# Block 0 of a hybrid decoder layer: the place of the first exponents on ScalarE and of the first own pairs on TensorE

## The reference

```python
q = (xb @ w_query).reshape(L, PEER_HEADS, 2, PEER_QUERY_DIM // 2)
s = jnp.einsum('lhpd,hpkd->lhpk', q, sub_keys)
vals, idx = lax.top_k(s, K)                       # 16 best of 128, per head and side
cand = (vals[..., 0, :, None] + vals[..., 1, None, :]).reshape(L, PEER_HEADS, K * K)
best, pos = lax.top_k(cand, K)
expert = jnp.take_along_axis(cidx, pos, axis=-1)  # 8 heads x 16 = 128 experts per token
gate = jax.nn.softmax(best, axis=-1)
h = jax.nn.gelu(jnp.einsum('ld,lhkd->lhk', xb, expert_u[expert]), approximate=False)
return jnp.einsum('lhk,lhkd->ld', (h * gate), expert_v[expert])
```

## Time and profile before

| | |
|---|---|
| median of 3 runs | 3099.26 us (3098.27 to 3103.0) |
| the profiled execution | 3094.55 us |
| its span | 3092.7 us |
| mean granted TensorE clock | 0.871 |
| TensorE busy | 2367.8 us (77%) |
| VectorE busy | 2240.8 us (72%) |
| ScalarE busy | 1122.2 us (36%) |
| GpSimd busy | 1195.3 us (39%) |
| moved by DMA | 1235.90 MB, mean 400 GB/s |

### The profile page before, as it was taken

The page is one execution under the profiler, slowest core; times in us unless marked ns, Lnnn a source line. Parts: engine busy times, 40 slices in busy tenths (PEclk is TensorE's granted clock), DMA queues, the critical chain, the costliest instruction groups (busy, mean ns, idle before and its releaser), DMA issues.

```text
span 3092.7 us, 37897 instructions
## 1 busy us (share of the span) xinstructions
PE 2367.8 (77%) x11834; PEld 1335.1 (43%) x11834; DVE 2240.8 (72%) x5649; ACT 1122.2 (36%) x3540; POOL 1195.3 (39%) x1028
## 2 busy tenths in 40 slices
PE   8987878868798677877878778876878767785655
PEld 7773435534366343543446443542435424251111
DVE  5577656986679766797668966699656976678745
ACT  4224533254323633235322353224523353323222
POOL 0024452344423444234532344334543344434442
PEclk9999889889889898998989898998988879787777
DMA  8289999999999999999999999999999999999998
GB/s 350 75 339 418 421 420 409 398 414 420 420 415 413 410 420 420 402 404 418 421 419 403 414 420 421 413 394 413 418 420 406 418 413 420 420 372 421 412 421 338
DMA packets 189144, 1235.90 MB, mean 400 GB/s; under 512 B 21768, under 2 KB 21896, under 8 KB 54800
## 3 DMA queue, kind: packets, MB, share of 16 engines
q0 software_dynamic: 147456, 1073.81, 84.1%
q1 hardware_dynamic: 39312, 154.58, 12.7%
q10 hardware_dynamic: 2176, 5.10, 0.4%
HBM read 1229.21 MB, written 4.19 MB: 399 GB/s over the span
## 4 chain that ended last, share of the span: by engine, by line
DVE 29%; PE 29%; DMA 27%; ACT 7%; issue 6%; POOL 3%; DVEq 0%; SPq 0%; POOLq 0%; ACTq 0%
DMA ring<-in_uv,expert_used 26%; PE expert_sum L1048 13%; DVE ring L1920 13%; PE bank L627 7%; POOL ring L553 3%; PE bank L634 2%; ACT diag L1392 2%; PE bank L616 2%; DVE conv L1554 1%; DVE arena L1534 1%; DMA chunk<-in_weights 1%; ACT arena L1183 1%; DVE arena L1853 1%; DVE arena L1856 1%; PE bank L765 1%
## 5 line engine op out<-in xcount | busy, mean ns | idle before, releaser
L553 POOL DMA_INDIRECT ring<-in_uv,expert_used x1024 | 1195.1, 1167 | 1866.8 <-PE expert_sum L1048 1421.3
L1048 PE MATMUL expert_sum<-ring,diag 128*64 128x512 f32 x4096 | 1195.0, 713 | 632.4 <-ACT diag L1392 631.0
L1920 DVE CUSTOM_DVE_ANT_0 ring<-ring,x_pair 128x1024 f32<-128x1024 f32 x1024 | 1227.6, 1222 | 487.7 <-DMA ring<-in_uv,expert_used 482.6
L1048 PEld LDWEIGHTS expert_sum<-ring,diag 128*64 128x64 f32 x4096 | 312.5, 155 | 1258.3 <-issue 1243.9
L1385 ACT ACTIVATE h_raw<-h_raw 128x2 f32<-128x2 f32 x512 | 104.2, 204 | 1452.2 <-DVE h_raw L1920 1451.6
L1392 ACT ACTIVATE diag<-const,h_raw 128x64 f32<-128x64 f32 x1024 | 292.7, 333 | 8.1 <-PE expert_sum L1048 8.1
L1388 ACT ACTIVATE h_raw<-h_raw,gate_used 128x1 f32<-128x1 f32 x1024 | 245.6, 286 | 16.7
L627 PEld LDWEIGHTS bank<-oT,chunk 128*128 128x128 f32 x1344 | 152.7, 192 | 22.7 <-issue 22.7
L627 PE MATMUL bank<-oT,chunk 128*128 128x128 f32 x1344 | 158.6, 277 | 0.0
L1534 DVE MAX8 arena<-arena 128x8 f32<-128x128 f32 (+1 forms) x384 | 104.2, 325 | 25.9 <-ACT arena L1331 19.8
L616 PE MATMUL bank<-chunk,oT 128*128 128x256 f32 x464 | 110.7, 389 | 0.0
(11 more groups left out here) (289 smaller groups left out, 2655.9 us busy)
## 6 DMA issues: line engine op xcount, KB each, us to landing
chunk<-in_weights SPq DMA_DIRECT2D x228, 512.0 KB, 8.6
ring<-in_weights SPq DMA_DIRECT2D x17, 1024.0 KB, 23.4
ring<-in_uv,expert_used POOLq DMA_INDIRECT x1024, 15.3
chunk<-in_weights SPq DMA_DIRECT2D x4, 1024.0 KB, 20.0
x<-in_x SPq DMA_DIRECT2D x8, 512.0 KB, 13.9
o_cat<-in_xT SPq DMA_DIRECT2D x7, 512.0 KB, 14.5
out<-oT ACTq DMA_DIRECT2D x7, 512.0 KB, 9.0
xT_even<-in_xT SPq DMA_DIRECT2D x4, 512.0 KB, 10.8
```

Source lines behind the costliest of these rows:

```text
L553: pool.indirect_dma_start(out=place(n, j), out_offset=None, in_=io["uv"], in_offset=bass.IndirectOffsetOnAxis(ap=expert_used[:, j:j + 1], ...
L1048: mm = pe.matmul(expert_sum[i][c * SPAN:(c + 1) * SPAN, :], diag[:, (j % DIAGS) * SPAN:(j % DIAGS + 1) * SPAN], place(n, j)[:, D + i * 512 ...
L1920: dve.tensor_tensor_reduce(u, u, x_pair[:, (j % 2) * D:(j % 2 + 1) * D], 1.0, 0.0, ALU.mult, ALU.add, h_raw[:, j:j + 1]).then_inc(dotted.s ...
```

## The change

Two edits, both for block 0 only. On ScalarE the exponents of the first 32 slots move from behind the fifth piece's key-score copy to ahead of the fourth's. On TensorE the own pairs of block 0 are taken at the same mark as on the other engines (b in place of b - 1), with 14 pairs as the most, so that the number of pairs added at the end of block 0 stays 14, as `after_own` (L1070) says for the later blocks.

```diff
@@ TensorE @@
             taken = [0]
-            mix(0, Marks(own=lambda a, b: experts(0, b - 1)), lambda n: None, early=True)
-            after_own = taken[0]
+            after_own = sum(OWN.values()) - 1
+            mix(0, Marks(own=lambda a, b: experts(0, min(b, after_own))), lambda n: None, early=True)
@@ ScalarE @@
                 mark("more0")
                 queries_out(later + 1)
                 mark("sel0")
+                if n == 0:
+                    exponents(1, slice(0, PART))
                 key_scores_out(later + 1)
                 mark("rest0")
                 if n:
...
                 queries_out(later + 2)
                 mark("pick0")
                 key_scores_out(later + 2)
-                if n == 0:
-                    exponents(1, slice(0, PART))
                 mark("top1")
```

## The result

The changed kernel takes 3108.55 us (median of 16 runs, 3100.26 to 3113.05) against 3099.59 us for the kernel before in the same runs (16 runs, 3092.76 to 3107.16). The ratio is 1.0023, 95% interval 1.0014 to 1.0033: 7.1 us slower (4.3 to 10.2). The forecast was 2 us slower: the direction held, the size did not. The result is 5.1 us above the forecast. Counted from no change it is 0.23%, just over the bound of 0.2%, and so in the part "slower", which had a chance of 0.16. 3099.26 x 1.0023 = 3106.4 us lies in the stated range of 3092 to 3108; the median itself, 3108.55, is half a microsecond above it.

The account below looks back on a forecast made before the run. DMA, full from the fifth slice on, was taken as the bound; a 7.9 us head start is given back in smaller gaps, leaving DMA 1 to 3 us behind, taken as +2: 3099.26 + 2 = 3101 us, range 3092 to 3108.

Parts of the forecast that it names:

- the six waits: Block 0's input pass: TensorE stands still for ScalarE's diagonals at six marks, 3.1 or 1.8 us each, 13.4 us together.
- pair 0 at 168.3: Start of block 0's input pass: TensorE can start own pair 0 at 168.3 us, 7.3 us earlier than before.
- the full clock behind its wait: TensorE's own pair 0 in block 0 runs at 2.4 GHz after standing still, 1.94 us in place of 3.68.
- What bounds the kernel: Whole kernel: DMA is full from the fifth slice on; its 9.8 us of idle time near the change is the most winnable.
- rival (b): First front of block 1: the pass's delay is not hidden and costs the whole 8.1 us, so 3107; chance 0.09.
- The prediction's sign of being wrong: DMA's share in the trace after: staying 1.0 from 172 to 270 us, or under 1.0 between 275 and 300.
- Part 1: ScalarE, block 0: earlier exponents cost nothing and end VectorE's 10.37 us wait; the last key-score copy and Gelu load come late next.
- Part 2: TensorE, block 0's input pass: pairs taken at VectorE's mark, 5.3 us ahead, then 13.4 of stalls; pair 13 ends at 276.6, not 268.5.
- rival (c): Block 0's input pass: the six stalls make TensorE's clock fall to 1.2 GHz, 10 us more on the pass, 3109; chance 0.06.
- What DMA makes of it: Gathers in block 0's input pass: DMA idles 14.0 us against 11.0, no gap until 186.1 after the first gathers; taken as +2.
- (a): Gathers in block 0's input pass: the gaps do not arise, the head start stays, 8 us kept gives 3091; chance 0.10.
- (d): Block 0: the TensorE edit does nothing by itself; the exponents alone bring at most 7 us, 3092; chance 0.07.

Follow-up runs that it names:

- the last version: The changed kernel with ScalarE making block 0's pairs ahead of its copies and TensorE taking none at mark top1: 3086.56 against 3101.52 us for the kernel before, ratio 0.9944.
- the second trace: The changed kernel, unedited, traced once more as a single execution: span 3098.7 us, DMA idle 15.5 us over 170 to 290 us.

## Why the prediction came out as it did

The direction came out for the reason given, the six waits. The size did not, and three steps failed, all in the reckoning of the start: pair 0 at 168.3, the full clock behind its wait, and no DMA idle time ahead of its places. All three made the changed kernel look faster than it is.

**What bounds the kernel**: right. The span of the profiled executions follows DMA's idle time one for one (the table). So block 1's later start cost nothing beyond it, and rival (b), a price for the delay of the pass as such, fell: the run with the TensorE edit alone delays the pass most (pair 13 ends at 293.4) and still lies on the same line. The prediction's sign of being wrong, a share under 1.0 between 275 and 300, did not come: the changed kernel has 1.00, 1.00, 0.99, 1.01 and 1.02 in the five windows of 5 us. What was too low is the bound on what can be won, 9.8 us: the last version won 17.4 (13.6 to 21.1). The bound was read from one execution of the kernel before, which lay 4.7 us below its median and had less idle time than the second one.

**Part 1**: right in kind. The exponents follow the fourth query copy without a wait of ScalarE; VectorE's idle time there fell from 10.37 to 1.81 us rather than to nothing, since that copy itself came at 157.04 and not 154.28, behind the gaps. What is late next was ScalarE's last key-score copy and the Gelu load, as forecast. The table load at 169.98 took 1.28 us and was followed by the first activation at 171.28. The Trainium skill ("ScalarE: Activation LUTs", What ACT_TABLE_LOAD costs) adds a drain of about 1.38 us to the load at every switch of tables; it does not show here either.

**Part 2**: the six waits were right in place and size (13.6 against 13.4 us). The step that failed is the start: "Pair 0 can start at 168.3" and "I take the full clock". Pair 0 started at 172.61, 4.3 us later, and took 3.68 us, at the half clock; pair 5 fell to the half clock too (3.62 us). So pair 13 ended at 278.10 + 5.37 = 283.5 and not at 276.6: 4.3 us for the start, 1.7 for pair 0's clock, 1.7 for pair 5's and some 0.4 for the step behind pair 0 and the six waits make 8.1, of which about 1 came back in shorter waits for weights (2.1 us against 3.0 before). The 4.3 us are the gaps and what they set back (the last key scores at 168.18 against 163.89). One of the two traces of the kernel before has the gaps too, so they are no cost of the change. Nor is pair 0's half clock a new cost: it was there before, behind the wait of 6.93 us, and so was the slow step behind the pair:

```profile
179.17 4.46 PE L627 MATMUL bank<-xT_even,chunk 128*128 128x128 f32 x32
```

It is a gain of 1.7 us that the sum counted and that did not come. The 1.7 us at pair 5 are new. They are what is left of rival (c), to which I gave 0.06: at one of its six waits the clock fell, not at all six.

The full clock was read from the earlier trace rows, 4 us of standing still with a grant of 1.00. That row is the middle of a longer wait. In the same trace the grant fell right behind it, and the pair took 3.68 us:

```profile
310.00:312.00 2.00, 0.45 (x2) 0.33 (x4) 1.42 (x4) 1.92 (x10) 0.00 (x0) 0.55 1.02 426
```

```profile
311.55 3.68 PE L1048 MATMUL expert_sum<-ring,diag 128*64 128x512 f32 x8 [6.03 <-ACT diag L1392]
```

So the row did not show that a pair behind such a wait has the full clock, neither for pair 0 nor against rival (c).

**What DMA makes of it**: right in kind, a size off. The reckoning had 14.0 us of idle time for the changed kernel; the traces have 18.0 and 15.5. The term that it put at nothing is the idle time ahead of pair 0's places: with pair 0 done at 170.2 "it has no gap until 186.1", but pair 0 was done at 176.3, and DMA was idle 4.9 us between 170 and 180 (3.5 in the second trace). Two more large gaps lie where the reckoning put them, before pair 2's and pair 5's places. The first is deeper as the half clock and the late pair 0 push pair 2's places to 195.96 (forecast 188.8), the second by pair 5's clock. Against the kernel before it is 18.0 - 10.6 = 7.4 us in the first traces, 15.5 - 12.8 = 2.7 in the second ones. The second pair, with the gaps on both sides, is close to the forecast of 2; of the first pair's 7.4 us some 2 (12.8 - 10.6) go with the gaps, which the kernel before lacks there. The measured 7.1 us comes from 16 executions of each kernel that were not looked into one by one, so its agreement with the first pair of traces may be luck.

**Rivals.** (a), the head start stays, fell: DMA's idle time grew. (d), the edit to TensorE does nothing by itself, erred most: alone it costs 12.7 us. For the exponents alone (d) gave at most 7 us; measured are 10.5 (6.5 to 14.6), in the spans 7.0. That the first edit by itself is the better kernel would have followed from the prediction's own step: with TensorE one mark behind, its first step covers the 3.2 us for which it has to wait for ScalarE. Each engine's order was looked at for the two edits together, and that comparison was not made.

What stays open: how the 7.1 us split between waits and clock, since the run that filled the first wait is inside the noise of the changed kernel; why both traced executions of the changed kernel (3101.53 and 3100.47 us) lie 7 to 8 us below its median, so that a typical one was not seen; and whether the best version's lead on the ScalarE edit alone is 7 us, as the ratios say, or nothing, as the two spans say.

## What to carry to other kernels

Where DMA is full for the rest of the kernel, price an early change by the DMA idle time it leaves in its own stretch, and take the starting point from several traces, not from one. A row that is to show what a wait does must reach to the wait's end and to the work behind it. An engine that runs one step behind its supplier is not only late: the step in between covers the supplier's own work, and it may be closed up only if the supplier's order is changed as well, so that what the consumer waits for comes ahead of the copies. When two edits come together, work out each alone: here one was worth -10.5 us and the other +12.7. An order in which ScalarE makes the pairs ahead of its copies, and TensorE takes them at their mark but for the first, was worth -17.4.

## What was not expected of the hardware

TensorE's clock behind a wait of 3.2 us is not settled by its length. After the four waits of 3.27 us ahead of pair 0 (in four traces) the pair took 3.68 us, the half clock (1.2 GHz) each time; after waits of 3.16 us it took 1.94 us in one place and 3.62 in another of the same trace. The windows of the changed kernel show one of the falls:

```profile
216.00:218.00 2.00, 0.00 (x0) 0.00 (x0) 1.97 (x7) 1.94 (x8) 0.04 (x1) 1.00 0.95 377
218.00:220.00 2.00, 1.11 (x4) 0.57 (x6) 1.94 (x4) 0.75 (x4) 0.00 (x0) 0.73 0.89 274
220.00:222.00 2.00, 2.00 (x7) 0.32 (x3) 1.89 (x6) 0.00 (x0) 0.00 (x0) 0.50 0.69 283
```

The grant is still 1.00 while TensorE stands still, falls as it starts again and holds at 0.50 through the pair. At pair 0 of the same trace it fell earlier, inside the wait:

```profile
170.00:172.00 2.00, 0.00 (x0) 0.00 (x0) 1.71 (x8) 1.96 (x5) 0.00 (x0) 0.78 1.01 406
```

The Trainium skill ("TensorE: Matmul & The Clock Gate", A second HAM failure mode) tells of a kernel in which frequent short idle stretches between groups of matmuls make the clock swing between its two levels. This trace agrees in part: the clock swung at two of seven such waits.

In 9 of the 10 traces TensorE has two or three gaps of 0.3 to 0.95 us at 153 to 158 us with nothing that it waits for. In the changed kernel's trace they come 8 us behind the start of the first gather (146.29), when DMA has just become full (share 0.93 over 148 to 150). Of the two traces of the kernel before, the one with the gaps has pair 0 4.5 us later. Their cause was not tested.
